# Moving the weight ring and the normed activations 64 bytes up in SBUF, in a streamed one-core encoder block

## The reference

```
h    = rmsnorm(x, g_pre_mix)
proj = h @ w_in                      # 2048 x 18448, split into the inputs of both mixers
y_m  = (sigmoid(m_o) * head_rmsnorm(mlstm(q, k, v, gates))) @ w_branch_m
y_a  = head_rmsnorm(diff_attention(q, k, v)) @ w_branch_a
x    = x + rmsnorm((g_m * y_m + g_a * y_a) @ w_out, g_post_mix)
h    = rmsnorm(x, g_pre_ffn)
u    = causal_dwconv(h @ w_up)       # 2048 x 11264
x    = x + rmsnorm((gelu(gate) * val) @ w_down, g_post_ffn)     # 5632 x 2048
```

## The kernel before

| tensor | first byte | remainder by 512 |
|---|---|---|
| raw, w_hi, w_lo | 16512, 32896, 49280 | 128 |
| h_hi, h_lo | 65664, 82048 | 128 |
| chan | 98432 | 128 |
| gm, hm_hi, hm_lo, ha_hi, ha_lo | 103488 and up | 64 |
| ks_hi, ks_lo | 209984, 214080 | 64 |

## Time and profile before

### The profile page before, as it was taken

The page is one execution under the profiler, slowest core; times in us unless marked ns, Lnnn a source line. Parts: engine busy times, 40 slices in busy tenths (PEclk is TensorE's granted clock), DMA queues, the critical chain, the costliest instruction groups (busy, mean ns, idle before and its releaser), DMA issues.

```text
span 1951.5 us, 36101 instructions
## 1 busy us (share of the span) xinstructions
PE 1907.3 (98%) x13774; PEld 1810.6 (93%) x13774; DVE 1099.8 (56%) x1287; ACT 897.4 (46%) x1159; POOL 75.0 (4%) x103
## 2 busy tenths in 40 slices
PE   6999999999999999999999998999999999999998
PEld 6999999989999999999999887999999999988886
DVE  5555446644664457444545556666666666655555
ACT  5444344533553455443343445545454445544443
POOL 5600000000000000000000001000000000000000
PEclk9999999999999999999999999999999999999999
DMA  6655455545455555555555663555555555565553
GB/s 208 197 171 170 152 175 170 179 146 184 155 181 162 166 169 173 173 186 190 191 188 191 241 219 119 178 182 184 183 182 183 182 182 183 176 221 188 190 193 140
DMA packets 166302, 351.48 MB, mean 180 GB/s; under 512 B 12916, under 2 KB 13517, under 8 KB 165581
## 3 DMA queue, kind: packets, MB, share of 16 engines
q1 hardware_dynamic: 165005, 344.40, 54.4%
q10 hardware_dynamic: 848, 4.79, 0.6%
q0 software_dynamic: 368, 1.09, 0.2%
HBM read 348.12 MB, written 2.12 MB: 179 GB/s over the span
## 4 chain that ended last, share of the span: by engine, by line
issue 59%; PE 39%; DVE 0%; POOL 0%; POOLq 0%; ACT 0%; DVEq 0%; ACTq 0%
PE ps L1112 12%; PE ps L1113 12%; PE ps L1114 12%; PE ps L1174 1%; PE ps L1247 1%; PE ps L1224 0%; POOLq L446 0%; PE ps L1182 0%; POOL stat L447 0%; PE ps L1223 0%; ACT gm L677 0%; PE ps L1230 0%; DVE gm L837 0%; DVE h_lo L809 0%; DVE xn L809 0%
## 5 line engine op out<-in xcount | busy, mean ns | idle before, releaser
L813 DVE TENSOR_TENSOR w_lo<-raw,w_hi 128x1024 fp32r<-128x1024 f32 x638 | 781.9, 1230 | 740.8 <-ACT w_hi L517 737.8
L517 ACT ACTIVATE w_hi<-raw 128x1024 fp32r<-128x1024 f32 x640 | 676.4, 1059 | 861.1 <-PE ps L1114 701.2
L1112 PE MATMUL ps<-h_hi,w_hi 128*128 128x256 f32 x3200 | 911.2, 285 | 12.8 <-issue 12.8
L1113 PE MATMUL ps<-h_lo,w_hi 128*128 128x256 f32 x3200 | 908.5, 284 | 0.0
L1114 PE MATMUL ps<-h_hi,w_lo 128*128 128x256 f32 x3200 | 908.4, 284 | 0.0
L1112 PEld LDWEIGHTS ps<-h_hi,w_hi 128*128 128x128 f32 x3200 | 617.3, 193 | 9.3 <-issue 8.7
L1113 PEld LDWEIGHTS ps<-h_lo,w_hi 128*128 128x128 f32 x3200 | 617.2, 193 | 5.5 <-issue 4.9
L1114 PEld LDWEIGHTS ps<-h_hi,w_lo 128*128 128x128 f32 x3200 | 617.3, 193 | 0.0
L1286 PE MATMUL ps<-w_hi,ks_hi 128*128 128x512 f32 x448 | 175.9, 393 | 0.2 <-DVE ks_lo L809 0.2
L1290 PE MATMUL ps<-w_lo,ks_hi 128*128 128x512 f32 x448 | 175.4, 392 | 0.0
L1286 PE MATMUL ps<-w_hi,ks_lo 128*128 128x512 f32 x448 | 138.5, 390 | 0.0
(11 more groups left out here) (166 smaller groups left out, 1378.3 us busy)
## 6 DMA issues: line engine op xcount, KB each, us to landing
raw<-in_w_in SPq DMA_DIRECT2D x288, 512.0 KB, 3.4
raw<-in_w_up SPq DMA_DIRECT2D x176, 512.0 KB, 4.5
raw<-in_w_down SPq DMA_DIRECT2D x88, 512.0 KB, 4.6
raw<-in_w_branch_m SPq DMA_DIRECT2D x32, 512.0 KB, 3.5
raw<-in_w_branch_a SPq DMA_DIRECT2D x32, 512.0 KB, 4.5
raw<-in_w_out SPq DMA_DIRECT2D x32, 512.0 KB, 4.6
x<-in_x ACTq DMA_DIRECT2D x1, 2048.0 KB, 12.7
gm<-in_x SPq DMA_DIRECT2D x3, 512.0 KB, 6.9
```

The lines of the kernel that those rows point to most:

```text
L517: return nc.scalar.activation(out_ap, in_ap, ACT.Copy, scale=scale)
L813: nc.vector.tensor_tensor(w_lo[:, slot, :], raw[:, slot, :], w_hi[:, slot, :].bitcast(F32), ALU.subtract).then_inc(lo_done, 1)
L1112: nc.tensor.matmul(out_ap, stat_hi, mov_hi, start=start, stop=False, skip_group_check=True)
L1113: nc.tensor.matmul(out_ap, stat_hi, mov_lo, start=False, stop=False, skip_group_check=True)
```

## The change

Two tensors that nothing reads or writes are declared, one of 64 bytes per partition ahead of `raw` and one of 448 bytes behind `h_lo`. `raw`, `w_hi`, `w_lo`, `h_hi` and `h_lo` each start 64 bytes later, at remainder 192 by 512. Everything from `chan` on starts 512 bytes later and keeps its remainder. No instruction is added, removed or moved.

```diff
--- before.py
+++ after.py
@@ -144,11 +144,13 @@
             return ctx.enter_context(nc.semaphore(name))
 
 
+        sb("ring_shift", [P, 16])
         raw = sb("raw", [P, RING, UNIT])
         w_hi = sb("w_hi", [P, RING, UNIT], F32R)
         w_lo = sb("w_lo", [P, RING, UNIT], F32R)
         h_hi = sb("h_hi", [P, KT, T], F32R)
         h_lo = sb("h_lo", [P, KT, T], F32R)
+        sb("ring_rest", [P, 112])
         chan = sb("chan", [P, C_ALL])
         shp = sb("shp", [P, S_ALL])
         stat = sb("stat", [P, 16])
```

## The result

The changed kernel takes 1969.42 us (median of 4 runs, 1967.28 to 1970.89), the kernel before 1956.44 us beside it. The ratio is 1.0069, with a 95% interval of 1.0055 to 1.0084: slower by 13 us, where 13 us less had been forecast, and outside the range.

What follows compares the result with a forecast made beforehand. TensorE, busy 98% of 1951.5 us, was taken to bound the kernel by number of matmuls times pace. 13.0 + 0.2 = 13.2 us off the 1956.0 us median gave 1942.8 us, range 1931 to 1965 us.

Steps and rivals of the forecast that it cites:

- The rival that the addresses do nothing here: Operand addresses do not set the matmul pace, the change is worth 0: 1956 us; chance 0.18, including effects that cancel.
- Step 1: Ring by `h`, both ways, 10368 matmuls: distance stays 0, so pace stays 120.0 and 226.7 ns, worth 0 us.
- Step 2: Ring stationary, `hm` and `ha` moving, 1536 matmuls, distance -64 to -128: excess stays 6.67 ns (16 cycles) each, 0 us.
- Step 3: `ks` stationary, ring moving, 512 columns, 1440 matmuls, distance +64 to +128: from 229.0 to 220.0 ns, 13.0 us less.
- Step 4: `hm` stationary, `h` moving, 48 gate matmuls, distance +64 to +128: from 117.9 to 113.3 ns, 0.2 us less.
- Step 5: ScalarE and VectorE splits and the loads use new remainders but stay covered; loads land in 4.6 us at worst.
- parity: Operands collide when starts are equal modulo 128: `hm` and `ha` +10.2 us, `ks`-stationary matmuls -3.3 us, 1963 us; chance 0.16.
- The place of the moving operand: The moving operand's place sets the pace, not the distance: about 1874 us, or 2025 us and over; chances 0.12 and 0.05.
- Less excess: Distance 128 has no excess at 256 columns, 1933 us; none at 512 columns either, 1923 us; chance 0.07.

## Why the prediction was wrong

*What bounds the kernel, and the reading of the rows:* right. The time is the number of matmuls by their pace, the pace goes with the distance of the operands, and no other engine comes near. The rival that the addresses do nothing here falls: moving `ks` alone by 448 bytes costs 0.36%. The Trainium skill (SBUF — State Buffer, section Who interferes with whom) calls TensorE's two read ports independent and says that it never waits on anyone; these runs differ from that, and the measurement decides.

*Step 1, ring by `h`, 0 us:* right. 10368 matmuls kept 120.0 and 226.7 ns. The shift of everything shows that the place alone does nothing.

*Step 2, `hm` and `ha` at -128, 0 us:* wrong. They went from 1 step to 1.8, +8.1 us. The step that failed is the choice of the value: "equality is the dearest at this width, this pair moves further from it". It took "further from 0" for "cheaper" on one pair of points. -64 has a pace, 113.3 ns, that no other distance tried has (-32: 118.3, -96: 117.3 or 118.7, -128: 118.7), so here the move away from it cost 5.3 ns a matmul.

*Step 3, rows at +128, -13.0 us:* wrong, and by sign. They went from 2.35 to 2.9 steps in the output and 3 in the down projection, +6.0 us, and this step carries 19 of the 27 us between forecast and result; step 2 carries the other 8. "Two places apart they should meet once or not at all" was a picture of how the streams meet, with no row under it. A row spoke against it and stood in the same list: at 512 columns distance 0 has 226.7 ns and +64 has 229.0, so there moving away from equality made it dearer. A line through the two points of that width would have put +128 at 231 ns, +3 us. What in the chip makes +128 dear stays open; that the distance makes it is shown by moving `ks` alone.

*Step 4, the gates:* the sign was wrong, the size nothing: from 117.9 to about 118.7 ns over 48 matmuls.

*Step 5, cover of splits and loads:* right. TensorE's waits are as before, ScalarE's for it grew. One reading in it was off: the 4.6 us in the earlier trace rows are the median time to landing of one group of loads, not the worst. Nothing in the sum rests on it.

*The rivals:* the slower one, parity, had the right sign and the right size for `hm` (+10.2 us forecast, +8.1 found) but the wrong reason. It asks for the pace of distance 0 at 128, and the rows have 226.7 ns at 0 and 233.3 at +128; it had them gaining 3.3 us where they lost 6.0. The place of the moving operand fell. Less excess fell too: no trace has it at ±128.

*The range:* its upper end, 1965 us, took the loss of `hm` from one rival with the rows' gain from the same. Both bounds of steps 2 and 3 stood in the text, +10.2 and +9.6 us, 1976 us together; they belonged in one case, since both rest on the same unseen distance.

## What to carry to other kernels

Where TensorE is bound and its pace is steady but over one column per cycle, tabulate the pace of each kind of matmul against the distance of its two operands modulo 256 bytes, each width by itself; here a few pads worth 2.2% stood behind that table. Interpolate nothing in it: measure a distance by moving one small operand alone, and keep groups whose paces are good at their distances. Repeat the run, for a distance can have two paces and one trace shows only what it drew. When one shift moves several groups to the same unseen distance, their bounds belong to one case and are added.

## What the runs showed of the hardware that was not expected

- The pace of back-to-back float32r matmuls depends on the addresses of stationary and moving operand relative to each other, from 113.3 to 120.0 ns at 256 columns and 226.7 to 233.3 at 512, all at a granted clock of 1.00. Moved together, the operands keep their pace (1954.93 against 1955.16 us), and so they do when the distances -64 and +64 grow to -320 and +320 bytes (1954.87 against 1955.8 us).
- Shifts of 32 bytes show (118.3 ns at -32 for 256 columns, 233.3 at +32 for 512 where 0 has 226.7), so it isn't whole 64-byte pieces.
- One distance can have two steady paces. A stretch keeps the one it has, for the 450 us measured of the up projection, and two turns of one loop can differ (22.62 and 21.78 us for the same 192 matmuls). Where two kinds follow each other without a pause their paces go together: 512 columns at +64 had 233.3 ns behind 117.8 and 228.8 behind 113.3, 24 times of 24 in three traces. In the kernel before, at distance 0 for most of the time, no second pace appeared. What picks one in the first place, and why the distance counts at all, these runs leave open.
